# Mixers of a two-block transformer: row projections of 512 columns in place of 256

## What is computed

```
h = rms_norm(x, attn_norm_w[layer])
proj = h @ w_in[layer]                      # (512, 1024) @ (1024, 3072)
a_q, a_i, a_zf, a_zb, a_g, b_u, c_q, c_k, c_v = split(proj)   # six of 256, three of 512
o_a = hgrn2_mixer(a_q, a_i, a_zf, a_zb, a_g)   # gated recurrence over positions, both directions
o_b = fourier_mixer(b_u)                       # 2-D DFT over positions and channels
o_c = dilated_attention_mixer(c_q, c_k, c_v)   # rotary on c_q and c_k
x = x + concat(o_a, o_b, o_c) @ w_out[layer]
```

## Time and profile before

| | us |
|---|---|
| median of 3 runs | 2207.17 (2206.57 to 2209.41) |
| span of the profiled execution | 2211.8 |
| PE busy | 2148.4 (97% of the span) |
| DVE busy | 1324.7 |
| ACT busy | 949.9 |
| POOL busy | 189.1 |

### The profile page before, as it was taken

One profiled execution on the slowest core, in us unless ns is written; L12 is line 12 of the kernel. 1 busy time (PEld: TensorE's weight loads), 2 busy tenths in 40 slices (PEclk: granted clock), 3 DMA queues, 4 the chain that ended last, 5 costly groups with the idle time before them and its releaser, 6 DMA issues.

```text
span 2211.8 us, 32932 instructions
## 1 busy us (share of the span) xinstructions
PE 2148.4 (97%) x13984; PEld 1681.6 (76%) x13984; DVE 1324.7 (60%) x1976; ACT 949.9 (43%) x1442; POOL 189.1 (9%) x159
## 2 busy tenths in 40 slices
PE   8998999999999999999999999999999998999997
PEld 6885688888888785788888885676888567777775
DVE  8886555335437867455255453857433454888887
ACT  5445532222234347432223332345221234888885
POOL 1220000000001310100000200000000001122220
PEclk9999999999999999999999999999999998999999
DMA  5222033322222231222222221212110443799985
GB/s 187 69 80 77 20 119 119 119 101 97 102 85 77 72 96 39 76 83 102 102 96 95 96 96 55 77 53 82 59 59 32 144 168 125 292 349 364 358 346 217
DMA packets 55000, 275.69 MB, mean 125 GB/s; under 512 B 13142, under 2 KB 13398, under 8 KB 26048
## 3 DMA queue, kind: packets, MB, share of 16 engines
q1 hardware_dynamic: 45344, 264.32, 33.0%
q0 software_dynamic: 8928, 8.33, 1.1%
q10 hardware_dynamic: 576, 0.87, 0.1%
HBM read 268.31 MB, written 29.36 MB: 135 GB/s over the span
## 4 chain that ended last, share of the span: by engine, by line
PE 86%; DVE 7%; ACT 3%; DMA 1%; issue 1%; SPq 0%; POOL 0%; POOLq 0%; DVEq 0%; ACTq 0%
PE psum L123 83%; PE psum L126 3%; DVE A_mix L136 2%; ACT A_mix L130 1%; DVE WL L136 1%; DMA A_moe<-h_rows,A_moe 1%; ACT A_mix L133 1%; DVE A_second L136 1%; DVE A_mix L156 0%; DVE A_second L144 0%; DVE A_mix L162 0%; ACT WH L130 0%; SPq L168 0%; DMA A_mix<-A_mix 0%; DVE HL L136 0%
## 5 line engine op out<-in xcount | busy, mean ns | idle before, releaser
L136 DVE TENSOR_TENSOR WL<-raw,WH 128x1024 fp32r<-128x1024 f32 x236 | 300.9, 1277 | 351.6 <-ACT WH L130 351.2
L130 ACT ACTIVATE WH<-raw 128x1024 fp32r<-128x1024 f32 x236 | 247.5, 1054 | 357.6 <-PE psum L123 341.7
L123 PE MATMUL psum<-HH,WH 128*128 128x512 f32 x736 | 301.6, 410 | 17.5 <-DVE HL L144 10.1
L123 PE MATMUL psum<-R_op,WH 128*128 128x512 f32 x1024 | 316.0, 390 | 0.0
L123 PE MATMUL psum<-R_ffn,WH 128*128 128x512 f32 x1024 | 315.1, 389 | 0.0
L123 PE MATMUL psum<-HH,WL 128*128 128x512 f32 x736 | 290.3, 394 | 0.0
L123 PE MATMUL psum<-HL,WH 128*128 128x512 f32 x736 | 290.2, 394 | 0.0
L123 PEld LDWEIGHTS psum<-R_op,WH 128*128 128x128 f32 x1024 | 192.2, 188 | 40.6 <-issue 1.0
L123 PEld LDWEIGHTS psum<-R_ffn,WH 128*128 128x128 f32 x1024 | 192.2, 188 | 39.9
L123 PE MATMUL psum<-R_moe 128*128 128x512 f32 x800 | 198.3, 404 | 5.8 <-DVE ring_moe L136 3.4
L123 PE MATMUL psum<-R_ffn,WL 128*128 128x512 f32 x512 | 199.2, 389 | 0.0
(11 more groups left out here) (206 smaller groups left out, 3000.1 us busy)
## 6 DMA issues: line engine op xcount, KB each, us to landing
ring_moe<-in_w_gu SPq DMA_DIRECT2D x64, 1024.0 KB, 10.1
raw<-in_w_in SPq DMA_DIRECT2D x41, 1024.0 KB, 5.0
raw<-in_w_up SPq DMA_DIRECT2D x32, 1024.0 KB, 4.9
raw<-in_w_down SPq DMA_DIRECT2D x32, 1024.0 KB, 4.9
ring_moe<-in_w_dn SPq DMA_DIRECT2D x32, 1024.0 KB, 6.8
raw<-in_w_out SPq DMA_DIRECT2D x12, 1024.0 KB, 4.9
kept<-A_second SPq DMA_DIRECT2D x20, 256.0 KB, 2.6
A_mix<-A_mix SPq DMA_DIRECT2D x64, 64.0 KB, 2.0
```

Source lines behind the costliest of these rows:

```text
L123: return self.raw.matmul(o, l, r, start=start, stop=stop)
L130: return self.raw.activation(o, i, f, scale=scale)
L136: return self.raw.tensor_tensor(o, a, b, op)
```

## The change

The four rows projections become two of 512 columns: a_i and b_u together, and c_v whole. Both stand at the end, behind c_q and c_k, so a mixer has ten projections. Their weights are laid out anew on the host (`w_row`: 512 columns of 4 row tiles to a chunk). A rows projection now has two chunks, so four units i = 0 to 3, each of two row tiles of 512 columns, and four banks, one for each group of 128 positions (tk 0 to 3). Its eight pieces are 12 matmuls of 512 columns each, in the order of `ROW_PIECES` (unit, first group). ACT empties the groups 2 and 3 one step before the groups 0 and 1 (`act_rows`). The rotary work moves with c_q and c_k (ROT 14 to 12), and on ACT and POOL the string of the weave has R14 two steps later. The DFT's first part waits for the groups 2 and 3 of c_v, its second part for the groups 0 and 1.

```diff
-                      lin([W[0, 0]], "silu", m.aq2, ly=ly), lin([W[4, 0]], "silu", m.ag2, ly=ly),
-                      lin([W[1, 0]], "rows", m.ai3, ly=ly)]
+                      lin([W[0, 0]], "silu", m.aq2, ly=ly), lin([W[4, 0]], "silu", m.ag2, ly=ly)]
...
-            m.tail += [lin([W[5, 0]], "rows", m.u3, ly=ly)]
-            m.tail += [lin([W[10 + j, 0]], "rows", m.cv3[:, :, 256 * j:256 * j + 256], ly=ly) for j in range(2)]
+            for j, to in enumerate(((m.ai3, m.u3), (m.cv3,))):
+                m.tail.append(lin([I["w_row"][ly, j, k] for k in range(2)], "rows", to, ly=ly))
...
-            for m in range(2):
-                b = (2 * (l.n - s2.low[0].n) + m) % 3 if l.kind in ("lat", "shift", "keep") else l.n % 2 * 2 + m
+            for m in range(4 if l.kind == "rows" else 2):
+                b = (2 * (l.n - s2.low[0].n) + m) % 3 if l.kind in ("lat", "shift", "keep") else (l.n % 2 * 2 + m) % 4
...
+        ROWS = (2, 3, 0, 1)
+
+        ROW_PIECES = ((0, 0), (1, 0), (0, 2), (1, 2), (2, 2), (3, 2), (2, 0), (3, 0))
+
         def pe_rows(e, l):
...
+            us = [chunks[n][2] + h for n in l.chunks for h in range(2)]
+            for i, tk0 in ROW_PIECES:
+                e.wait_ge(*at("w_lo", us[i]))
+                wh, wl = unit(us[i])
+                for tk in (tk0, tk0 + 1):
+                    if i == 0:
+                        clear(e, l, tk)
+                    o, ts = bank_of(l, tk), slice(tk * 128, (tk + 1) * 128)
+                    for k in range(2):
+                        xh, xl, made = operand(l, 2 * i + k)
+                        e.wait_ge(*at(*made))
+                        ws = slice(k * 512, (k + 1) * 512)
+                        e.mm(o, xh[:, ts], wh[:, ws], i + k == 0, False)
+                        e.mm(o, xl[:, ts], wh[:, ws], False, False)
+                        t = e.mm(o, xh[:, ts], wl[:, ws], False, i == 3 and k == 1)
+                    if i == 3:
+                        t.then_inc(*did("lin_mm", l.n, tk))
+                    elif tk == (3, 3, 1)[i]:
+                        t.then_inc(*did("w_use", us[i]))
+                yield
...
+        def act_rows(e, l, tks):
+            e.wait_ge(*at("nrm_dve", 2 * l.ly - 1, "col"))
+            for tk in tks:
+                ps, w = bank_of(l, tk), S // len(l.to)
+                e.wait_ge(*at("lin_mm", l.n, tk))
+                for i, to in enumerate(l.to):
+                    t = e.act(to[:, tk, :], ps[:, i * w:(i + 1) * w], ACT.Copy, rcol[:, tk:tk + 1])
+                t.then_inc(*did("lin_act", "ps", l.n, tk))
+
         def act_made(e, l):
 
+            if l.kind == "rows":
+                act_rows(e, l, ROWS[2:])
+                return
...
+                        if made is act_made and l.kind == "rows" and (n, h) == (l.chunks[-1], 1):
+                            act_rows(e, l, ROWS[:2])
                         u = chunks[n][2] + h + 2
...
-            e.wait_ge(*at("lin_act", "ps", x.head[4].n, 1))
+            e.wait_ge(*at("lin_act", "ps", x.tail[4].n, 1))
...
-                    l = x.tail[-1 if part else -2]
-                    e.wait_ge(*emptied(l, 1))
-                    e.wait_ge(*emptied(x.tail[-1], 1))
+                    e.wait_ge(*emptied(x.tail[-1], 1 if part else 3))
...
-        ROT = 14
+        ROT = 12
...
-        MIX = "u" * 12 + "c" + "uu" + "cucuu" * 8 + "cuu" * 4 + "cuuuc"
+        MIX = "u" * 12 + "c" + "uu" + "cucuu" * 6 + "uu" + "ccu" + "cucuu" + "cuu" * 4 + "cuuuc"
...
+    a["w_row"] = np.stack([lay(np.concatenate([w[:, 256:512], w[:, 1280:1536], w[:, 2560:3072]], 1), 4, 512)
+                           for w in (g["w_in"][i] for i in range(2))])
```

More of the change, by code:

```diff
@@ L606, in act_made @@
                     e.act(sg, sg if l.kind == "gate" else l.to[:, m, :], ACT.Sigmoid).then_inc(*did("lin_act", "sg", l.n, m))
[L607 to L613, removed]
                 elif l.kind == "copy":
@@ L1494, in win_dve @@
             for i, also in ((21, fold), (22, fold_again)):
-                steps[f"s{i}"] = lambda i=i, also=also: (rot_dve(e, x, i - ROT), also(e, x))
+                steps[f"s{i}"] = lambda also=also: also(e, x)
             yield from between(dve_lins(e, x.head + x.tail, True), **steps)
```

## The result

The kernel after takes 2220.28 us in the median (four runs, 2218.05 to 2225.03), the kernel before 2206.87 on the same chip (four runs, 2205.01 to 2209.41). The ratio is 1.0056 with an interval of 1.0039 to 1.0073: slower by 12.4 us (8.6 to 16.1). The forecast was 2214.3 with a range up to 2219.5; the ratio's interval on 2207.2 gives 2215.8 to 2223.3. The direction held; the size came out some 5 us above the sum, at the upper edge of the stated range.

What follows compares the result with a forecast made beforehand. PE, busy 97% of the span, was taken as the bound, through its work and its waits. -4.8 - 4.1 + 12.6 + 3.4 = +7.1 us on 2207.2 gave 2214.3, range 2206.5 to 2219.5 (forecast's own 2210.5 to 2218).

Steps and rivals of the forecast that it cites:

- rival C: Clock falls at both P34 and P38, for longer, costing 1.5 and 3.0 us a mixer: +12.7, 2219.9; chance 0.12.
- Term 1: Rows projections on PE: 384 fewer matmuls save 5.1 us, less 0.3 lost before P21: -4.8 us.
- The part lost at P21: Wait before P21 hangs on earlier ACT and DVE work, so some matmul gain is lost: +0.3 us, both mixers.
- Term 2: PE's waits at R16 (0.34), R21 (0.69) and the DFT's first part (1.02) end in both mixers: -4.1 us.
- Term 3: New PE waits for low parts of units 17 at P34 (2.3) and 19 at P38 (4.0), both mixers: +12.6 us.
- rotary two units earlier: Rotary steps and SP loads move earlier; unit 18 and R14's exponentials some 2 us later, counted as costing nothing.
- edits at nothing: Changed PSUM emptying, banks and rotary placement were counted as zero, with thin covers at P41 and R20.
- Term 4: Half clock behind P38's wait costs 1.7 us a mixer (bounds 0 and 3.0), none at P34: +3.4 us.
- Rival B: The waits at P34 and P38 come but the clock holds: +3.7 us, 2210.9; chance 0.20.
- The covers at P41 and R20: ACT's emptying about 0.4 us ahead of P41, 0.3 ahead for R20; up to 0.5 each if lost.
- The base: Sum made against the profiled span of 2211.8, 4.6 above the median; difference carried over to the median 2207.2.

Runs made afterwards that it cites:

- kernel 1: Kernel after, with the first rows projection's pieces (a_i, b_u) in unit order as before the change; 2209.79 us, 1.0007 of the kernel before.
- kernel 2: Kernel after, with only the last four pieces of the first rows projection reordered, so unit 19 is wanted in P39; 2208.3 us, 1.0010 of the kernel before.
- kernel 7: kernel 1 with the rotary work back where it was before the change (ROT = 14, swaps behind the next chunk load); 2204.24 us, 0.9977 of the kernel before.
- kernel 8: kernel 7 with ACT's steps 39 and 40 (emptying a_i and b_u) before R18; 2203.32 us, 0.9972 of the kernel before.
- kernel 9: kernel 8 with DVE's R20 (states) before its steps 41 and 42, ahead of the rotary step; 2203.10 us, 0.9978 of the kernel before.
- kernel 6: Kernel after, with sixteen unread 512-column matmuls filling PE's wait before P38 in both mixers; 2215.61 us, 1.0031 of the kernel before.
- kernel 3: Kernel after, with only the first four pieces of the first rows projection reordered, so unit 17 is wanted in P35; 2218.13 us, 1.0048 of the kernel before.
- kernel 10: Second traced execution of the kernel after with ACT's split of unit 19 moved before R16, nothing else changed; 2210.12 us.
- kernel 11: Third traced execution of the kernel after with ACT's split of unit 19 moved before R16, nothing else changed; 2210.32 us.

## Why the prediction was right, and where it was short

The sign and the cause hold: the two demands moved up by one piece cost more than the narrower work saves, and kernels 1 and 2 show it by taking them back. The number is less good than it looks. 1.0056 on 2207.2 is 2219.5, the very end of the stated range, and that end was set by rival C, half of whose mechanism (a fall at P34) did not happen. The forecast's own range, 2210.5 to 2218, misses it. That range also does not follow from its stated bounds: P34 at 0.7 to 3.5 and the clock at 0 to 3.0 give 2207.7 to 2219.3. That the result still lies inside is partly luck.

**Term 1, fewer matmuls (-4.8): right as a mechanism, sized too large.** 512 columns with h stationary start every 0.229 us beside the 0.2268 assumed, which alone takes 0.8 us off. The whole can be read from the traces by the time from a mixer's first projection matmul to the DFT's first, less PE's waits of 0.25 us and more between them. Before it is 175.63 - 3.39 = 172.24 us in the first mixer and 173.18 - 3.42 = 169.76 in the second. In kernel 1 it is 175.67 - 5.15 = 170.52 and 173.04 - 5.14 = 167.90, in kernel 7 173.11 - 2.74 = 170.37 and 170.54 - 2.79 = 167.75, all at full clock: 3.6 and 3.9 us less for both mixers, where 5.1 was forecast. The part lost at P21 was sized at 0.3; the waits there grew by 1.72 - 1.34 = 0.38 and 1.45 - 1.34 = 0.11, together 0.5.

**Term 2, waits that end (-4.1): right.** All three are gone, the DFT's worth was measured alone, and kernels 8 and 9 confirm that R21 hangs on the rotary step in front of the states. Whether the earlier rotary work alone would have ended R21's wait is not shown: in the kernel after PE comes late anyway, and in kernel 7 the wait is absent with the rotary work late, since P41's wait comes first.

**Term 3, new waits (+12.6): right in place, one missed.** P38: 4.0 predicted, 3.98 measured, from the chain R16, copies, high part, low part. P34: 2.3 predicted, 1.76 measured, but P33 waits 1.07 just before. Together 2.83: low part 17 came at 124.66 + 1.22 = 125.88 as forecast (125.72), and PE without P33's wait would have been at P34 at 124.17 - 1.07 = 123.1. So the sum in each mixer was mis-sized by 0.5 only. The step that was wrong is "rotary two units earlier" among the edits at nothing: I costed its DMAs on SP's queue and its product in front of low part 17, but not that it delays the exponents on which ACT's exponentials, and behind them the split of unit 16, wait. In the kernel after that costs little, since P34 would wait anyway; it costs P33, R14 and R16 once the order of pieces is mended: 2 x (1.07 + 0.73 + 0.82 - 0.28) = 4.7 us by the idle times, 6.6 by kernel 7 against kernel 1.

**Term 4, the clock (+3.4): right in kind, mis-sized.** I took 1.7 us a mixer from the nearest idle time, 3.43 us. Held against kernel 6's trace it was 2.4 and 2.15, between that and the bound of 3.0 from the earlier trace rows: 4.5 for both where the term has 3.4. It is not a fixed price: kernel 3's first mixer paid 1.4 for the same wait. Rival B (the clock holds) falls, and C in part: half clock for longer at P38, but full at P34.

**The covers at P41 and R20.** Called thin, 0.4 and 0.3 us. In the kernel after they hold, because PE loses 4.0 + 2.4 us at P38. Kernels 1, 2 and 7 have PE there in time, and P41 waits 1.0: ACT is then 1 us late, not 0.4 ahead. That cover was P38's own wait.

**The sum again.** From the mixer's first projection matmul to the DFT's first, the kernel after takes 180.76 and 178.45 us, the kernel before 175.63 and 173.18: +5.13 and +5.27, together +10.4. The waits of the projections are +10.0 of it (8.53 and 8.27 in the two mixers, in place of 3.39 and 3.42), the clock +4.5, so that -4.1 is left for the matmuls, near the 3.6 and 3.9 above. +10.4 is inside the 8.6 to 16.1 measured; the forecast had +7.1. Of the difference of 3.3 us, 1.1 is clock, 1.2 is waits (1.0 at P33 and P34, 0.2 at P21), 1.0 is matmuls. The 2 us between +10.4 and the ratio's +12.4 were not traced.

**The base.** Spans of the two profiled executions differ by 5.6 us only. The kernel before had the clock at half in both attentions in that execution, and the kernel after did not. The stretch of the first attention, before and then after:

```profile
195.00:215.00 20.00, 16.78 (x101) 8.82 (x101) 14.42 (x44) 14.25 (x33) 0.00 (x0) 0.91 0.23 86
```

```profile
195.00:215.00 20.00, 15.50 (x80) 7.98 (x80) 15.73 (x41) 13.95 (x29) 0.00 (x0) 1.00 0.15 52
```

Nothing in the change touches this place. Carrying the terms over to the median, rather than expecting the spans to differ by their sum, was the right choice, and a comparison of the two spans alone would have called the prediction too high. The same two traces give +10.4 where only the changed part is compared.

The Trainium skill (TensorE: Matmul & The Clock Gate, "What's actually happening") lets the clock follow how busy the engine has recently been, between two levels. Kernel 6 agrees: with the same wait and PE kept busy the clock did not fall. The fixed part of 2.5 ns that the same page ("Back-to-back issue gap") gives for an isolated matmul does not describe the new pieces either: 0.229 us for 512 columns at 2.4 GHz leaves 16 ns.

## What to carry to other kernels

When a reordering saves work on the bounding engine, list for each piece the first moment at which it wants each operand, and hold that against the moment of delivery in the old trace; here the order of pieces moved two demands up by one piece, and taking that back (kernel 1) returned 10.8 of the 12.4 us lost. A wait hides others: after each repair look for what is late next, because of 16.7 us removed on paper 5.2 were taken over by waits that had been covered. The best kernels here (7 to 9) keep the wide pieces and the DFT's earlier start, use units in their old order and leave the rotary work where it was: 0.9972 to 0.9978 of the time before.

## What was not expected of the hardware

The clock also fell behind idle times of PE of about 2 us, but not always. It fell for 3.4 us behind 2.26 us of idle time in kernel 10, behind 1.94 us at P21 in kernel 8 and behind 1.92 there in kernel 11, and not behind 1.92 at another place in the kernel before nor behind 1.76 at P34. In the first attention of the kernel before it was at half for 3.4 us with waits of 1.40 and 1.06 us around it; the kernel after has the same two waits there and no fall. The stretches at P21 in kernel 8:

```profile
76.70:78.10 1.40, 1.32 (x5) 1.14 (x6) 1.40 (x4) 1.02 (x1) 0.00 (x0) 0.91 0.00 0
78.10:81.50 3.40, 3.40 (x10) 2.58 (x10) 3.40 (x6) 0.00 (x0) 0.00 (x0) 0.53 0.15 24
```

The fall came about 1.1 us after PE had taken up work again: PE started at 76.78, and the share of 0.91 up to 78.10 means half clock from about 77.85. In kernel 10 it was 1.1 us too. Such falls are not in the same places in all executions of one kernel, and they go with the time: the four runs after with granted clocks of 0.989, 0.989, 0.988 and 0.985 took 2218.05, 2219.19, 2221.37 and 2225.03 us. With this spread, differences under about 2 us could not be told apart with twelve runs each.
